# The seam between mixer and MLP: when the MLP's weights are fetched, and where its first tile is normalised

## The chip, the cores and the metric

The kernel runs on the 8 cores of one Trainium2 chip, as one program with other data on each core; cores don't talk to each other. A core takes half of one sequence: 4096 output tokens, with 2064 tokens of lookback. The metric is device time in microseconds, of the slowest core. Of a core's engines, TensorE (PE) multiplies matrices, ScalarE (ACT) and VectorE (DVE) do pointwise work and empty PE's eight PSUM banks, GpSimd (POOL) does pointwise work in SBUF alone and issues the DMAs that convert f32 weights to bf16, and SyncE (SP) issues all other DMAs. Each engine takes its instructions in the order in which they were written; they wait for one another by semaphores.

## The reference

```
h = rms_norm(x, norm_mix_g)
a_b, a_c, a_v, q, k, v, g_a, g_b = split(h @ w_in)
y_a = (a_b * causal_dwconv(a_c * a_v)) @ w_proj_a
y_b = dilated_window_attention(q, k, v) @ w_proj_b      # 12 heads, three dilations
x = x + (sigmoid(g_a + b_0) * y_a + sigmoid(g_b + b_1) * y_b) @ w_out
h = rms_norm(x, norm_ffn_g)
gate, val = split(causal_dwconv(h @ w_up))              # 3 taps, 2 x 2816 channels
x = x + (silu(gate) * val) @ w_down
out = rms_norm(x, final_norm_g)
```

Here x is (4, 8192, 1024) in f32, w_up is 1024 x 5632 and w_down 2816 x 1024.

## The kernel before

The program has three stages: attention with its projections, the mixer's rest, and the MLP. The last two run over the same nine token tiles: one of 388 tokens (4 of them lookback), three of 384 and five of 512 (`BW`; `BB[j]` are tile j's blocks of 128 tokens).

**The mixer's rest**, for each tile j: `conv_c` for four channel chunks, then `gate_oc` for eight output chunks oc. One `gate_oc` is 26 matmuls (L652) into four PSUM banks, two sigmoids on ACT (L1217), two multiplies on DVE (L1231) and a sum into mT on POOL (L1234). Then `wout` multiplies mT with w_out (L1263), DVE adds x (L1267), and SP stores the sum to `x1_d` in HBM (L1271). Tiles overlap: the first conv chunk of tile j+1 is written ahead of `wout(j)`. The last tile, j = 8, has nothing behind its `wout`.

**The MLP**, for each tile: 22 times `c_pair` (up-projection of a gate and a value chunk, 2 x 8 matmuls, L652 by the helper `fm`; ACT scales with the bias, L1411; DVE adds the two other taps, L1418; silu on ACT, L1429, written one pair late; product on POOL, L1431, into `actT`), then `c_down` (L1469) for each block, first k = 0 to 19 of both halves, then k = 20 and 21. Seven buffers tmpC go round among the pairs. The input of a tile is normalised in three steps for each block: `c_stat` (square on ACT, L417, and 1/sqrt in six small steps on POOL, L322 to L330), `c_mul` (DVE, L425, which frees the buffer xn for SP's next load of x1, L1344), and `c_back` (eight transposes on PE, L437, and one copy on DVE, L441, into h2T). For tiles 1 to 8 these steps are hooks within the tile before; for tile 0 they stand ahead of the loop, behind the load and the scaling of g2 (L1330, L335), and behind them stand load and scaling of g3 and the loads of x1 for `c_down` (L1381).

**Weights and memory.** The MLP's weights stay in SBUF: w_up in eleven pieces wU0 to wU10, each two DMAs of 512 KB (as bf16) by `wu_load` (L1162); w_down in three pieces wD0 to wD2 (k = 0 to 7, 8 to 15, 16 to 21) by `wd_load` (L310). All are issued by POOL. SBUF is one arena in which later buffers are laid over earlier ones; `Sched` makes the first user of a buffer wait for the last users of all that lay there. wU0 to wU2 are loaded in tile 1. wU3 to wU5 lie over the conv weights and are issued in tile 8 after its last `conv_c`; wU6 to wU9 lie over the gate weights, and wU6 to wU10 are issued after the last `gate_oc` of tile 8; wD0 to wD2 lie over w_proj_a, w_proj_b, w_out and mT and are issued after `wout(8)`. actT lies over the attention's output and over the buffers xB from which x1 is stored.

Of the kernel before, what the change touches and what calls it, by code (L numbers as in the profile page):

```python
# [8 lines left out]
F32 = mybir.dt.float32  # L9
BF16 = mybir.dt.bfloat16  # L10
# [4 lines left out]
D = 1024  # L15
KC = 8
# [114 lines left out]
def build_program():  # L131
# [94 lines left out]
    R1 = 0  # L226
# [927 lines left out]
    wu_off = [R4, R4 + 8192, R4 + 16384, R1, R1 + 8192, R1 + 16384, R2, R2 + 8192, R2 + 16384, R2 + 24576, R5]  # L1154
# [13 lines left out]
    def wd_load(p):  # L1168
        k0, kn = wd_k[p]
        wD[p] = buf("wD%d" % p, R3 + k0 * 2048, [128, kn, D], BF16)  # L1170
        wload(wD[p], w_dn[k0 * 128:(k0 + kn) * 128, :].rearrange("(k p) c -> p k c", p=128), ("wD%d" % p,))
# [103 lines left out]
    for _ in range(4):  # L1275
        xb_load()
    conv_c(0, 0)
    for j in range(9):
        for c in range(1, 4):
            conv_c(j, c)  # L1280
        if j == 0:
            while ub_b[0] < len(BB[0]) + 1:
                tickno[0] += 1
                ub_step(True)
        if j == 8:
            for p in (3, 4, 5):
                wu_load(p)
        if j == 1:
            for p in (0, 1, 2):
                wu_load(p)  # L1290
        for oc in range(8):
            gate_oc(j, oc)
        b_done[0] = j
        if j + 1 < 9:
            need_b = 1 + sum(len(BB[q]) for q in range(j + 2))
            if j + 2 < 9:
                hb_load(j + 2)
            conv_c(j + 1, 0)
            wout(j)
            while ub_b[0] < need_b:  # L1300
                tickno[0] += 1
                ub_step(True)
        else:
            for p in (6, 7, 8, 9, 10):
                wu_load(p)
            wout(j)
    while deferred:
        tickno[0] += 1
        for d in list(deferred):
            if d[0] <= tickno[0]:  # L1310
                deferred.remove(d)
                d[1]()
    for p in range(3):
        wd_load(p)


    actT = buf("actT", W, [128, 22, 512], BF16)
    tmpC = [buf("tmpC%d" % i, W + 22528 + i * 2048, [128, 512], F32) for i in range(4)]
    h2T = buf("h2T", W + 31232, [128, KC, 512], BF16)
# [4 lines left out]
    g3b = buf("g3b", W + 68096, [128, D], F32)  # L1324
    tmpC += [buf("tmpC%d" % (4 + i), W + 72192 + i * 2048, [128, 512], F32) for i in range(3)]
# [4 lines left out]
    S.add("sp", lambda e: e.dma_start(out=g2b, in_=g2_d.partition_broadcast(128)), writes=[("g2b",)], dma_sem=sem_g2)  # L1330
    scale_g(g2b, ("g2b",))
    tmp_set["n"] = 7
# [162 lines left out]
    xn_load()  # L1495
    xn_load()
    for _ in range(1 + len(BB[0])):
        c_stat()
        c_mul()
        c_back()  # L1500
    S.add("sp", lambda e: e.dma_start(out=g3b, in_=g3_d.partition_broadcast(128)), writes=[("g3b",)], dma_sem=sem_g3)
    scale_g(g3b, ("g3b",))
    for _ in range(3):
        xr_load()
    for j in range(9):
        if j > 0:
            c_corr(j)
        for p in range(22):
            c_pair(j, p)
            if j + 1 < 9 and p in (11, 15):  # L1510
                c_stat()
            if j + 1 < 9 and p in (13, 17):
                c_mul()
# [186 lines left out]
```

How the kernel before makes its waits and increments, by code:

```python
    def emit_stream(ename, handle, tail=None):  # L1587
        waited = {}
        for op in S.ops[ename]:
            need_ = {}
            for d in op.deps:
                sem, val = d.ev
                if waited.get(id(sem), 0) < val and need_.get(id(sem), (None, 0))[1] < val:
                    need_[id(sem)] = (sem, val)
            for sem, val in need_.values():
                handle.wait_ge(sem, val)
                waited[id(sem)] = val
            ins = op.fn(handle)
            if op.dma_sem is not None:
                ins.then_inc(op.dma_sem, 16)
            elif op.signal:
                ins.then_inc(op.ev[0], 1)
        if tail:
            for sem, val in tail:
                handle.wait_ge(sem, val)
```

## Time and profile before

| what | value |
|---|---|
| median of 3 runs | 2178.29 us (2174.97 to 2178.88) |
| profiled execution | 2176.07 us |
| its span, slowest core (7) | 2174.5 us |
| spans of the 8 cores | 2160.0 to 2174.5 us |
| mean granted clock of the cores | 0.975 to 0.979 |
| PE busy | 2000.5 us (92%) |
| DVE, ACT, POOL busy | 1231.0, 859.3, 687.1 us |

The span runs from the first to the last instruction of the slowest core. The views used below are: the page, which cuts the span into 40 slices of 54.4 us with busy shares in tenths; the timeline of one engine, in which equal instructions are merged and the idle time before a row stands in brackets with what ended it; windows, with busy time of each engine in a stretch, the granted TensorE clock (1.0 is 2.4 GHz, 0.5 is 1.2 GHz), the share of the DMA engines and GB/s; the waits, who waited for whom; the chain, which goes back from the last instruction to what released each step; and the DMA views.

### The profile page before, as it was taken

The page shows a single profiled execution, that of the slowest core. Times are in us where ns is not written, and L with a number is a line of the kernel's source. Part 1 is how long each engine was busy: PE and PEld are TensorE (multiplying, and loading weights), DVE is VectorE, ACT ScalarE, POOL GpSimd, SP SyncE. Part 2 cuts the span into 40 slices and gives each one's busy share as a digit, 9 for nine tenths or more (in the row PEclk, how much of TensorE's full clock was granted, in tenths as well). Part 3 has the DMA queues.
Part 4 walks back from the last instruction along what each step waited for, and adds up shares of the span by engine and source line. Part 5 has one row for each costly group of instructions (what it writes and reads, how often), then busy time and mean ns, then how long its engine had stood idle before and what let it go on. Part 6 is the DMA issues. An engine that isn't in the chain of part 4 may idle for free.

```text
span 2174.5 us, 38060 instructions; the slowest of 8 cores (2160.0 to 2174.5 us)
## 1 busy us (share of the span) xinstructions
PE 2000.5 (92%) x11550; PEld 1038.2 (48%) x11550; DVE 1231.0 (57%) x1948; ACT 859.3 (40%) x1796; POOL 687.1 (32%) x1434
## 2 busy tenths in 40 slices
PE   3889989958999999999996499999999999999998
PEld 1546645534555544444442255555544444444443
DVE  5546665455444445344342387686777676858583
ACT  2456654452122221211211264464555453636261
POOL 4333251032111110111122244454545343535342
PEclk9999999988999999999998699999999999999999
DMA  9775857595372223123066921212010202020201
GB/s 182 147 150 146 187 155 124 115 181 143 108 151 74 72 72 127 36 92 105 1 133 111 199 54 69 69 37 71 30 69 30 88 20 97 21 97 20 78 2 49
DMA packets 124160, 201.70 MB, mean 93 GB/s; under 512 B 9620, under 2 KB 86170, under 8 KB 123576
## 3 DMA queue, kind: packets, MB, share of 16 engines
q1 hardware_dynamic: 81912, 164.99, 26.2%
q0 software_dynamic: 42048, 34.26, 12.1%
q8 instruction: 98, 1.61, 0.3%
q14 instruction: 102, 0.84, 0.1%
HBM read 172.86 MB, written 60.63 MB: 107 GB/s over the span
## 4 chain that ended last, share of the span: by engine, by line
PE 81%; DVE 5%; issue 5%; DMA 3%; POOL 2%; ACT 2%; SPq 1%; DVEq 0%; POOLq 0%; ACTq 0%
PE ps L652 56%; PE ps L1469 13%; PE ps L1263 5%; PE ps L658 3%; PE ps L437 1%; PE ps L528 1%; DVE arena L425 1%; DMA u_d<-arena 1%; DMA arena<-x_loc 1%; PE ps L553 1%; DMA arena<-v_d 1%; PE ps L1106 1%; DVE arena L1092 1%; POOL rtmp L328 1%; ACT arena L417 1%
## 5 line engine op out<-in xcount | busy, mean ns | idle before, releaser
L652 PE MATMUL ps<-arena 128*128 128x512 bf16 (+4 forms) x6848 | 1348.9, 357 | 6.5 <-ACT arena L255 4.3
L652 PEld LDWEIGHTS ps<-arena 128*128 128x128 bf16 x6848 | 659.3, 98 | 648.1 <-issue 16.8
L1418 DVE SCALAR_TENSOR_TENSOR arena<-ps,fcw_s,arena 128x511 f32<-128x511 f32 (+4 forms) x792 | 525.0, 687 | 106.3 <-ACT uc L1409 29.8
L1469 PE MATMUL ps<-arena 128*128 128x512 bf16 x1408 | 311.3, 379 | 4.4 <-POOL arena L1422 2.8
L1411 ACT ACTIVATE arena<-ps,fcb_s,fcw_s 128x512 f32<-128x512 f32 (+1 forms) x396 | 284.6, 731 | 0.3 <-ACT uc L1409 0.2
L1431 POOL TENSOR_TENSOR arena<-arena 128x512 bf16<-128x512 bf16 (+1 forms) x198 | 210.5, 1063 | 96.1 <-ACT uc L1409 60.5
L417 ACT ACTIVATE arena<-arena 128x1024 bf16<-128x1024 f32 (+1 forms) x114 | 119.9, 1052 | 299.5 <-DVE arena L1475 205.1
L1231 DVE TENSOR_TENSOR arena<-ps,arena 128x512 f32<-128x512 f32 (+2 forms) x144 | 90.6, 632 | 247.2 <-PE ps L652 240.3
L1469 PEld LDWEIGHTS ps<-arena 128*128 128x128 bf16 x1408 | 136.2, 98 | 166.6 <-issue 9.7
L1217 ACT ACTIVATE arena<-ps,bg_s 128x512 f32<-128x512 f32 (+2 forms) x144 | 92.1, 640 | 264.2 <-PE ps L652 264.2
L1234 POOL TENSOR_TENSOR arena<-arena 128x512 bf16<-128x512 f32 (+2 forms) x72 | 83.3, 1157 | 276.9 <-DVE arena L1231 243.0
L1429 ACT ACTIVATE arena<-arena 128x512 bf16<-128x512 f32 (+1 forms) x198 | 115.2, 582 | 113.1 <-POOL arena L1422 96.4
L425 DVE SCALAR_TENSOR_TENSOR arena<-arena,rstd 128x1024 bf16<-128x1024 f32 (+1 forms) x82 | 105.0, 1280 | 78.0 <-POOL rstd L330 77.7
L1422 POOL TENSOR_TENSOR arena<-arena,corr 128x2 f32<-128x2 f32 x352 | 84.3, 242 | 202.5 <-DVE arena L1418 190.8
L531 ACT ACTIVATE arena<-ps 128x512 bf16<-128x512 f32 x192 | 109.9, 595 | 79.0 <-PE ps L553 45.7
L255 ACT ACTIVATE arena<-ps 128x512 bf16<-128x512 f32 (+4 forms) x157 | 85.8, 548 | 135.2 <-PE ps L652 88.1
L437 PE MATMUL ps<-ident,arena 128*128 128x128 bf16 (+2 forms) x656 | 53.0, 227 | 92.2 <-DVE arena L425 55.5
L322 POOL TENSOR_SCALAR ssq<-ssq 128x1 f32<-128x1 f32 (+1 forms) x106 | 24.9, 235 | 347.6 <-ACT arena L417 297.2
L658 PE MATMUL ps<-arena 128*128 128x256 bf16 (+2 forms) x688 | 119.4, 322 | 1.3 <-DVE arena L441 1.3
L535 DVE TENSOR_TENSOR arena<-arena,mask 128x512 bf16<-128x512 bf16 x160 | 75.0, 476 | 80.1 <-ACT arena L531 78.5
L1263 PE MATMUL ps<-arena 128*128 128x512 bf16 (+1 forms) x528 | 117.7, 382 | 2.5 <-POOL arena L1234 2.5
L1475 DVE TENSOR_TENSOR arena<-ps,arena 128x512 f32<-128x512 f32 x64 | 44.1, 690 | 131.4 <-PE ps L1469 125.2
(89 smaller groups left out, 1276.5 us busy)
## 6 DMA issues: line engine op xcount, KB each, us to landing
arena<-x_loc SPq DMA_DIRECT2D x80, 512.0 KB, 5.4
arena<-x_d SPq DMA_DIRECT2D x64, 512.0 KB, 3.8
x_d<-arena SPq DMA_DIRECT2D x32, 512.0 KB, 4.8
out<-arena SPq DMA_DIRECT2D x32, 512.0 KB, 2.7
u_d<-arena SPq DMA_DIRECT2D x96, 132.0 KB, 5.8
arena<-u_d SPq DMA_DIRECT2D x32, 396.0 KB, 3.6
arena<-w_up POOLq DMA_DIRECT2D x22, 512.0 KB, 17.9
arena<-w_in POOLq DMA_DIRECT2D x10, 1024.0 KB, 22.4
```

What stands on the lines that cost most here:

```text
L417: S.add("act", lambda e: e.activation(out=junk[0:n, :], in_=xap[0:n, :], func=AF.Square, accum_out=ssq[0:n, col:col + 1]), reads=[xkey] + ...
L425: S.add("dve", lambda e: e.scalar_tensor_tensor(out=hbap[0:n, :], in0=xap[0:n, :], scalar=rstd[0:n, col:col + 1], in1=gb[0:n, :], op0=ALU. ...
L531: S.add("act", lambda e: e.activation(out=PA[pi], in_=ps[sbk], func=AF.Exp, scale=0.125), reads=[("ps", sbk)], writes=[("PA%d" % pi,)])
L652: S.add("pe", lambda e, kc=kc: e.matmul(out, lhsT=wap[:, kc, col0:col0 + 128], rhs=rhs(kc), start=(kc == 0), stop=(kc == kcn - 1), skip_gr ...
L658: S.add("pe", lambda e, kc=kc: e.matmul(out, lhsT=lhs(kc), rhs=wap[:, kc, c0:c0 + n], start=(kc == 0), stop=(kc == KC - 1), skip_group_che ...
L1217: S.add("act", lambda e, b=b, t=t, br=br: e.activation(out=tmp[t][:, 0:w_], in_=ps[b][:, 0:w_], func=AF.Sigmoid, bias=bg[:, br * 8 + oc:br ...
L1263: S.add("pe", lambda e, b=b, kc=kc, hf=hf: e.matmul(ps[b][0:n, :], lhsT=mT[:, kc, c0:c0 + n], rhs=wO[:, kc, hf * 512:(hf + 1) * 512], star ...
L1411: S.add("act", lambda e, b=b, t=t, ch=ch, w2_=w2_: e.activation(out=tmpC[t][:, 0:n], in_=ps[b][:, o:w_], func=AF.Identity, scale=w2_, bias ...
L1418: S.add("dve", lambda e, b=b, t=t, sh=sh, wv_=wv_, lo=lo: e.scalar_tensor_tensor(out=tmpC[t][:, lo:n], in0=ps[b][:, o + lo - sh:w_ - sh], ...
L1429: S.add("act", lambda e: e.activation(out=actT[:, p, 0:n], in_=tmpC[tg][:, 0:n], func=AF.Silu), reads=[("tmpC%d" % tg,)], writes=[("actT", ...
L1431: S.add("pool", lambda e: e.tensor_tensor(out=actT[:, p, 0:n], in0=actT[:, p, 0:n], in1=tmpC[tv][:, 0:n], op=ALU.mult), reads=[("tmpC%d" % ...
L1469: S.add("pe", lambda e, b=banks[hf], k_=k_, kk=kk, wt=wt, hf=hf: e.matmul(ps[b], lhsT=actT[:, k_, bi * 128:(bi + 1) * 128], rhs=wt[:, kk, ...
```

## The change

The buffers and helper functions of the MLP's normalisation are defined ahead of the mixer's loop, so that tile 8 can call them. h2T moves to R5, where tile 7's input lay; wU10 moves to where tile 8's input lay; g3b and two tmpC move. In tile 8, g2 and the first two parts of x1 are loaded after the last `conv_c`, and the normalisation of the MLP's tile 0 is spread over the `gate_oc` calls: after chunk 1 g2 is scaled and two `c_stat` run, after chunk 2 two `c_mul`, and so on by the list of letters (s, m and b for `c_stat`, `c_mul` and `c_back`). wU6 and wU7 are issued after chunk 4, wU8 to wU10 and wD0 after chunk 7, wD1 and wD2 after `wout(8)`. g3 and the x1 blocks for `c_down` are loaded after pair 3 of the MLP's tile 0, and g3 is scaled after pair 20. The bodies of the functions that move are as they were.

```diff
-    wu_off = [R4, R4 + 8192, R4 + 16384, R1, R1 + 8192, R1 + 16384, R2, R2 + 8192, R2 + 16384, R2 + 24576, R5]
+    wu_off = [R4, R4 + 8192, R4 + 16384, R1, R1 + 8192, R1 + 16384, R2, R2 + 8192, R2 + 16384, R2 + 24576, W + 31232]
...
+    actT = buf("actT", W, [128, 22, 512], BF16)
+    tmpC = [buf("tmpC%d" % i, W + (68096 + i * 2048 if i < 5 else 26624 + (i - 5) * 2048), [128, 512], F32) for i in range(7)]
+    h2T = buf("h2T", R5, [128, KC, 512], BF16)
+    hbC = [buf("hbC%d" % i, W + 39424 + i * 2048, [128, D], BF16) for i in range(2)]
+    g2b = buf("g2b", W + 43520, [128, D], F32)
+    xn = [buf("xn%d" % i, W + 47616 + i * 4096, [128, D], F32) for i in range(2)]
+    xr = [buf("xr%d" % i, W + 55808 + i * 4096, [128, D], F32) for i in range(3)]
+    g3b = buf("g3b", W + 22528, [128, D], F32)
+    sem_g2, sem_g3 = newsem("s_g2"), newsem("s_g3")
+    sem_xn = [newsem("s_xn%d" % i) for i in range(2)]
+    sem_xr = [newsem("s_xr%d" % i) for i in range(3)]
+    sem_out = [newsem("s_out%d" % i) for i in range(3)]
+    xn_list = [(0, -1)] + [(j, b) for j in range(9) for b in BB[j]]
+    xn_l, cf, cb = [0], [0], [0]
...
@@ -1285,11 +1349,22 @@
         if j == 8:
             for p in (3, 4, 5):
                 wu_load(p)
+            S.add("sp", lambda e: e.dma_start(out=g2b, in_=g2_d.partition_broadcast(128)), writes=[("g2b",)], dma_sem=sem_g2)
+            xn_load()
+            xn_load()
         if j == 1:
             for p in (0, 1, 2):
                 wu_load(p)
         for oc in range(8):
             gate_oc(j, oc)
+            if j == 8:
+                if oc == 1:
+                    scale_g(g2b, ("g2b",))
+                if oc == 4:
+                    wu_load(6)
+                    wu_load(7)
+                for k_ in ("", "ss", "mm", "bbs", "ms", "bm", "b", "")[oc]:
+                    {"b": c_back, "m": c_mul, "s": c_stat}[k_]()
         b_done[0] = j
...
         else:
-            for p in (6, 7, 8, 9, 10):
+            for p in (8, 9, 10):
                 wu_load(p)
+            wd_load(0)
             wout(j)
...
-    for p in range(3):
-        wd_load(p)
-
-
-    actT = buf("actT", W, [128, 22, 512], BF16)
-    tmpC = [buf("tmpC%d" % i, W + 22528 + i * 2048, [128, 512], F32) for i in range(4)]
-    h2T = buf("h2T", W + 31232, [128, KC, 512], BF16)
-    hbC = [buf("hbC%d" % i, W + 39424 + i * 2048, [128, D], BF16) for i in range(2)]
-    g2b = buf("g2b", W + 43520, [128, D], F32)
-    xn = [buf("xn%d" % i, W + 47616 + i * 4096, [128, D], F32) for i in range(2)]
-    xr = [buf("xr%d" % i, W + 55808 + i * 4096, [128, D], F32) for i in range(3)]
-    g3b = buf("g3b", W + 68096, [128, D], F32)
-    tmpC += [buf("tmpC%d" % (4 + i), W + 72192 + i * 2048, [128, 512], F32) for i in range(3)]
-    sem_g2, sem_g3 = newsem("s_g2"), newsem("s_g3")
-    sem_xn = [newsem("s_xn%d" % i) for i in range(2)]
-    sem_xr = [newsem("s_xr%d" % i) for i in range(3)]
-    sem_out = [newsem("s_out%d" % i) for i in range(3)]
-    S.add("sp", lambda e: e.dma_start(out=g2b, in_=g2_d.partition_broadcast(128)), writes=[("g2b",)], dma_sem=sem_g2)
-    scale_g(g2b, ("g2b",))
+    wd_load(1)
+    wd_load(2)
     tmp_set["n"] = 7
...
-    xn_load()
-    xn_load()
-    for _ in range(1 + len(BB[0])):
-        c_stat()
-        c_mul()
-        c_back()
-    S.add("sp", lambda e: e.dma_start(out=g3b, in_=g3_d.partition_broadcast(128)), writes=[("g3b",)], dma_sem=sem_g3)
-    scale_g(g3b, ("g3b",))
-    for _ in range(3):
-        xr_load()
     for j in range(9):
         if j > 0:
             c_corr(j)
         for p in range(22):
             c_pair(j, p)
+            if j == 0 and p == 3:
+                S.add("sp", lambda e: e.dma_start(out=g3b, in_=g3_d.partition_broadcast(128)), writes=[("g3b",)], dma_sem=sem_g3)
+                for _ in range(3):
+                    xr_load()
+            if j == 0 and p == 20:
+                scale_g(g3b, ("g3b",))
```

## Rows read from the trace of the kernel before

**Rows 1.** The page's slices: TensorE's granted clock in 40 slices of 54.4 us.

```profile
PEclk9999999988999999999998699999999999999999
```

**Rows 2.** PE timeline, 1080 to 1300: start, duration, instruction, count, idle before and its end.

```profile
1101.36 60.60 PE L652 MATMUL ps<-arena 128*128 128x512 bf16 x280
1164.48 15.44 PE L1263 MATMUL ps<-arena 128*128 128x512 bf16 x64 [2.52 <-POOL arena L1234]
1208.15 0.35 PE L437 MATMUL ps<-ident,arena 4*128 4x4 bf16 x8 [28.23 <-DVE arena L425]
...
1227.11 1.01 PE L437 MATMUL ps<-ident,arena 128*128 128x128 bf16 x8 [3.28 <-DVE arena L425]
1229.07 60.13 PE L652 MATMUL ps<-arena 128*128 128x388 bf16 x352 [0.94 <-DVE arena L441]
1289.22 4.26 PE L1469 MATMUL ps<-arena 128*128 128x512 bf16 x19
1294.08 5.36 PE L1469 MATMUL ps<-arena 128*128 128x512 bf16 x23 [0.60 <-POOL arena L1431]
```

**Rows 3.** Windows: stretch, length, busy PE, PEld, DVE, ACT, POOL, clock, DMA share, GB/s.

```profile
1140.00:1160.00 20.00, 20.00 (x94) 9.11 (x93) 4.46 (x7) 4.91 (x8) 5.05 (x4) 1.00 0.19 27
...
1200.00:1230.00 30.00, 4.32 (x36) 3.06 (x37) 7.38 (x8) 2.30 (x4) 9.24 (x26) 0.50 1.14 179
```

**Rows 4.** Waits, 1160 to 1230: who waited for what, total us, times, longest.

```profile
ACT arena L335 <- DMA arena<-g: 31.6, 1, 31.6
ACT arena L417 <- DMA arena<-x_d: 25.1, 3, 21.2
```

**Rows 5.** The chain, 1180 to 1420: start, duration, what.

```profile
1211.56 9.90 DMA arena<-x_d
...
1244.30 40.96 PE ps L652 x248
...
1299.44 0.47 PE ps L437 x8
```

**Rows 6.** POOL timeline, 1080 to 1240: DMA issues and one sum.

```profile
1120.10 5.31 POOL L1162 DMA_DIRECT2D arena<-w_up  x6 [0.55 <-issue]
...
1146.13 1.26 POOL L1234 TENSOR_TENSOR arena<-arena 128x512 bf16<-128x512 f32 x1 [4.35 <-DVE arena L1231]
...
1164.17 6.18 POOL L1162 DMA_DIRECT2D arena<-w_up  x7
1176.85 1.76 POOL L1162 DMA_DIRECT2D arena<-w_up  x2 [6.50 <-issue]
1194.78 0.88 POOL L1162 DMA_DIRECT2D arena<-w_up  x1 [16.17 <-issue]
...
1202.33 1.71 POOL L310 DMA_DIRECT2D arena<-w_dn  x2 [5.79 <-issue]
```

**Rows 7.** DMA queues, 1164.2 to 1262.2: q0 POOL's, q1 SP's; packets, MB, share.

```profile
q0 software_dynamic: 13264, 11.01, 83.7%
q1 hardware_dynamic: 2024, 7.36, 23.2%
```

**Rows 8.** Line L310, 1195 to 1205: the three w_dn pieces.

```profile
DMA to landing us min/median/max: 40.7/51.6/59.0
```

**Rows 9.** Line L1162, 1119 to 1126: the six pieces of wU3 to wU5.

```profile
DMA to landing us min/median/max: 7.7/15.3/19.8
```

**Rows 10.** Line L1344, 1180 to 1229: loads of x1.

```profile
DMA to landing us min/median/max: 8.4/9.9/12.1
```

**Rows 11.** Line L1271, 1165 to 1183: the last four stores of x1.

```profile
DMA to landing us min/median/max: 7.9/8.1/10.0
```

**Rows 12.** DVE timeline, 1180 to 1296: its first and last work in MLP tile 0.

```profile
1239.97 3.11 DVE L1418 SCALAR_TENSOR_TENSOR arena<-ps,fcw_s,arena 128x384 f32<-128x384 f32 x5 [11.05 <-ACT uc L1409]
...
1287.75 8.81 DVE L1418 SCALAR_TENSOR_TENSOR arena<-ps,fcw_s,arena 128x384 f32<-128x384 f32 x14
```

**Rows 13.** Lines, DVE, 1229 to 1297: group, count, busy us, mean ns, idle before.

```profile
L1418 DVE SCALAR_TENSOR_TENSOR arena<-ps,fcw_s,arena 128x384 f32<-128x384 f32 x87 | 50.0, 613 | 15.9 <-ACT uc L1409 11.1 <-DVE arena L1418 0.5
```

More of the change, by code:

```diff
@@ L1273, in wout @@
             later(3, xb_load)
[L1275 to L1303, printed above, removed]
-            for p in (6, 7, 8, 9, 10):
[L1305 to L1312, printed above, removed]
-    for p in range(3):
-        wd_load(p)
     actT = buf("actT", W, [128, 22, 512], BF16)
-    tmpC = [buf("tmpC%d" % i, W + 22528 + i * 2048, [128, 512], F32) for i in range(4)]
-    h2T = buf("h2T", W + 31232, [128, KC, 512], BF16)
+    tmpC = [buf("tmpC%d" % i, W + (68096 + i * 2048 if i < 5 else 26624 + (i - 5) * 2048), [128, 512], F32) for i in range(7)]
+    h2T = buf("h2T", R5, [128, KC, 512], BF16)
     hbC = [buf("hbC%d" % i, W + 39424 + i * 2048, [128, D], BF16) for i in range(2)]
@@ L1329, in build_program @@
     sem_out = [newsem("s_out%d" % i) for i in range(3)]
-    S.add("sp", lambda e: e.dma_start(out=g2b, in_=g2_d.partition_broadcast(128)), writes=[("g2b",)], dma_sem=sem_g2)
-    scale_g(g2b, ("g2b",))
-    tmp_set["n"] = 7
     xn_list = [(0, -1)] + [(j, b) for j in range(9) for b in BB[j]]
@@ L1382, in xr_load @@
               reads=[("x1_d", blk)], writes=[("xr%d" % sl, 0), ("xr%d" % sl, 1)], dma_sem=sem_xr[sl])
+    for _ in range(4):
+        xb_load()
+    conv_c(0, 0)
+    for j in range(9):
+        for c in range(1, 4):
+            conv_c(j, c)
+        if j == 0:
+            while ub_b[0] < len(BB[0]) + 1:
+                tickno[0] += 1
+                ub_step(True)
+        if j == 8:
+            for p in (3, 4, 5):
+                wu_load(p)
+            S.add("sp", lambda e: e.dma_start(out=g2b, in_=g2_d.partition_broadcast(128)), writes=[("g2b",)], dma_sem=sem_g2)
+            xn_load()
+            xn_load()
+        if j == 1:
+            for p in (0, 1, 2):
+                wu_load(p)
+        for oc in range(8):
+            gate_oc(j, oc)
+            if j == 8:
+                if oc == 1:
[5 more added lines that the diff above has]
+                    {"b": c_back, "m": c_mul, "s": c_stat}[k_]()
+        b_done[0] = j
+        if j + 1 < 9:
+            need_b = 1 + sum(len(BB[q]) for q in range(j + 2))
+            if j + 2 < 9:
+                hb_load(j + 2)
+            conv_c(j + 1, 0)
+            wout(j)
+            while ub_b[0] < need_b:
+                tickno[0] += 1
+                ub_step(True)
+        else:
+            for p in (8, 9, 10):
+                wu_load(p)
+            wd_load(0)
+            wout(j)
+    while deferred:
+        tickno[0] += 1
+        for d in list(deferred):
+            if d[0] <= tickno[0]:
+                deferred.remove(d)
+                d[1]()
+    wd_load(1)
+    wd_load(2)
+    tmp_set["n"] = 7
     fw = fcw.rearrange("p (c k) -> p c k", k=3)
```

## The prediction

> **What bounds the kernel now.** I read the page's slices first: TensorE's (PE's) granted clock stands at nine tenths or more but for two places, slices 9 and 10 (in the attention, which the change leaves alone) and slices 22 and 23, where the digits fall to 8 and 6 [rows 1]. Then PE's own timeline of the second place. The last mixer tile's output projection (L1263) ends at 1164.48 + 15.44 = 1179.92 us, and the first matmul of the MLP (L652) starts at 1229.07: 49.15 us in which PE does only four small groups of transposes [rows 2]. Third, the windows: from 1200 to 1230 PE is busy 4.32 of 30 us and its granted clock is 0.50, which is the 1.2 GHz level; in the gates of the last mixer tile (1140 to 1160) PE is full while VectorE (DVE), ScalarE (ACT) and GpSimd (POOL) are each busy about 5 of 20 us [rows 3]. Fourth, the waits of 1160 to 1230: ACT waits 31.6 us for one load of g2 and 25.1 us for loads of x1, and all else queues behind that [rows 4]. So the hole is a serial prologue (load, square, rstd, multiply, transpose) that starts only after the mixer has ended, with its loads in the thick of the weight stream. Nothing after the hole waits for anything else: the first down-projection starts at 1289.22, straight behind the last up-projection [rows 2].
>
> **The change, part by part.** The sum is made against the profiled execution (span 2174.5 us, 2176.07 us with what lies around it).
>
> *The prologue leaves the hole.* It moves between the gates of tile 8, where the three helper engines are three quarters idle. With its result in h2T before the output projection, the MLP's first matmul needs wU0 (loaded in tile 1), h2T and a free PSUM bank, so it can follow L1263 at once: minus 49.15 us. The transposes stay PE work: three groups of eight at 0.47 us at full clock [rows 5], and the four-row group at 0.35 at most (that was at half clock) [rows 2]: plus 1.8 us.
>
> *The clock.* PE restarted cold in 1229. At full clock 248 matmuls of tile 0 took 40.96 us, 0.1652 each [rows 5]; 352 of them make 58.1 us where 60.15 passed from 1229.07 to 1289.22 [rows 2]. Minus 2.0 us. The small wait of 2.52 us ahead of L1263 stays.
>
> *What the moved steps wait for in tile 8.* One output chunk of the gates is 26 of the 280 matmuls of 60.60 us, 5.63 us [rows 2]; chunk 2 ends at about 1134, chunk 3 at 1139.5, chunk 5 at 1151, chunk 6 at 1157. x1 blocks 1 and 2 are loaded once the first two multiplies have freed xn, at about 1136 and 1137.3. In the hole such loads landed after 8.4 to 12.1 us beside the weight stream [rows 10], and from a landing (1211.56 + 9.90) to the transposes (1227.11) 5.65 us passed [rows 2, 5]. So block 1 is ready for PE at 1150 to 1154, against PE's arrival at 1151.5; block 2, with four wU issues of 0.9 us [rows 6] ahead of it on POOL, by 1158.6 at the latest, against 1157.6. PE waits 0 to 3 us; I take 1. Queued behind ACT's wait for block 1 are the sigmoids of chunk 4, up to 6 us late; PE has eight banks, two chunks or 11 us, before it notices. On POOL the sum for mT of chunk 5 slips by 2 to 4 us, needed only at the output projection. On SP nothing is due between the xn loads and the stores of 1170. With that cover gone (loads over 15 us late) the whole delay would stand on PE.
>
> *The weight stream.* Before: wU6 to wU10 and wD0 to wD2 are issued from 1164.17 on, POOL being held up three times (at 1170, 1178 and 1196, the last issue at 1203.2) [rows 6], and the last piece lands 59.0 us after that, at 1262.2 [rows 8]; that was hidden, since the down-projection began at 1289. After, it begins at 1240, so this cover shrinks to nothing and the stream has to be sized. From 1164.2 to 1262.2 the POOL queue moved 11.01 MB and SP's queue 7.36 MB [rows 7], together 187 GB/s. After: wU6 and wU7 (2.1 MB) are issued behind the sum at 1146.13 [rows 6], when the stream of wU3 to wU5 (last landing 19.8 us after 1124.5, [rows 9]) is over, and are through by about 1166 to 1169. From there remain 8.9 MB of weights; of SP's 7.36 MB the loads of g2 and of five x1 blocks (3.1 MB) are gone from this stretch, leaving 4.2. 13.1 MB at 187 GB/s are 70 us: the last piece lands at 1236 to 1239. It is needed at k = 16 of the first down-projection: 1181.7 + 58.1 + 3.5 = 1243.3. Zero, with 4 to 7 us to spare. The bounds: at the 131 GB/s of the w_up pieces alone (six of 0.52 MB in 24.3 us, [rows 6, 9]) it lands at 1269 and costs 26 us; no bound below zero, since an earlier landing gains nothing. I take zero because 187 is the rate of just this mix.
> The Trainium skill speaks for the other end. "DMA: Bandwidth & Descriptors", section "Anatomy of one DMA", has a POOL-issued transfer cost 2 us plus its bytes at 436 GB/s; worked out from that as an estimate, the 13.1 MB would be through 30 us after 1166, at 1196. The trace does not agree (187 GB/s in this mix), and the measurement decides; by the page the first rival below would have no chance at all.
>
> *POOL's queue.* The order of the 13 pieces is unchanged. Before, seven went out one behind another, and then POOL was held up before the eighth, tenth and twelfth [rows 6]: seven under way seem to be what the queue takes. After, pieces 1 to 4 are through by 1169, so wU10 and wD0 go out by then, and wD1 and wD2 when L1263 has ended, about 1182 to 1184, with seven under way at most. Behind them on POOL stands the first gate product of the MLP, not due before 1188. Zero; if a piece held POOL until 1197, seven tmpC buffers and eight banks (eight pairs, 21 us) would hide it.
>
> *The start of the MLP.* Its first silu writes actT over xB and so waits for the last x1 store; stores landed after 7.9 to 10.0 us [rows 11], the last one issued near 1182.6, so by 1192.6, when ACT could have gone on at 1187. Before, ACT waited too (for g3): DVE's first operation came at 1239.97, 10.9 us after PE's start, and it then worked to 1287.75 + 8.81 = 1296.56 nearly without a gap (87 x 0.613 us) [rows 12, 13]; the price was 0.60 us on PE [rows 2]. After, DVE starts 3 us behind PE, pauses 5, but PE is 2 us faster: about as far behind at the end. g3's load and scaling come later and are needed only at the end of the down-projection. Bounds 0 to 3 us more than before; I take 0.5.
>
> **Sum:** -49.15 + 1.8 - 2.0 + 1.0 + 0.5 = -47.85 us. The profiled execution would take 2128.2; its 2176.07 stands 2.2 under the median 2178.29, which would become 2130.4 us.
>
> **Rivals.**
> *1. The weights come late.* PE then stands at k = 0, 8 or 16 of the first down-projection until wD0, wD1 or wD2 lands. For it: the slack is 4 to 7 us in 74; that wU6 and wU7 don't get ahead, because loads of x1 share their stretch, is the way in which the change would not do what it says. Against: the rate used already contains waits of POOL. At 160 GB/s the last piece lands at 1250, 7 us late: 2138. At the bound of 131: 2156.
> *2. The hooks hold PE in tile 8.* Loads of x1 at 12 us or more, one behind another, with the square, the rstd chain and the wU issues in order on ACT and POOL: 3 to 10 us, and PE's clock falls for a while: 2133 to 2141. For it: the bare 0 to 1 us of margin above. Against: PE's eight banks, and engines a quarter busy.
> *3. No gain: the chain only moves.* That needs a transfer which ends the hole whatever comes before it. The only candidate, the stream, ended 27 us ahead of the down-projection (1262.2 against 1289.2), so at least that part of the hole is not the stream's. 2178.
> *4. Slower.* The stream beside the kernel's own stores falls well below what rows show on the whole: if the 8.9 MB of weights and 4.2 MB of the rest go at under 105 GB/s, the last piece lands 125 us after 1166, at 1291 or later, PE stands 48 us in the first down-projection, goes cold there, and the gain is used up: at 95 GB/s 138 us, 61 us late, about 2191. Nothing but short stretches of the profile runs so low.
>
> **How the numbers follow.** Forecast 0.74 (2126 to 2134), rival 1 0.14 (2134 to 2156, mostly to 2142), rival 2 0.07, rival 3 0.015, rival 4 0.025, and 0.01 for a better end than the forecast's. The range 2124 to 2141 holds the forecast and the likelier part of rivals 1 and 2: its low end is the longest step saved with no stall at all, and the ordinary spread of runs. About 0.2% is what can be told from no change: faster 0.96, same 0.015, slower 0.025.
>
> **What would show it.** PE's timeline must have L652 straight behind L1263, with four groups of L437 among the gates and no gap over 3 us there; the granted clock at 1.0 from the first L652 of the MLP on; 352 matmuls of tile 0 in 58 us; the first L1469 about 60 us after the end of L1263, with idle time before it put down to DVE or POOL, not to w_dn. The POOL rows must show w_up issues near 1147, and the last w_dn landing before the first down-projection. A wait of L1469 for a DMA means rival 1; idle time of PE before L437 or L652 in tile 8 means rival 2. If the hole is gone and the time is not lower by 40 us or more, the forecast is wrong.

## The result, and the profile after

The changed kernel takes 2125.08 us (median of 4 runs, 2122.13 to 2130.84) against 2178.59 us (4 runs, 2174.97 to 2179.42) for the kernel before: ratio 0.9761, 95% interval 0.9735 to 0.9786. That is 5.3 us under the predicted 2130.4 and inside the range of 2124 to 2141. The comparisons here and below leave out the runs in which one half of the chip was disturbed.

The profiled execution took 2122.13 us, its span 2120.6 us on the slowest core (core 1); the eight cores spanned 2109.4 to 2120.6 us. PE is busy 1994.3 us, 94% of the span, and the granted clock of the cores is 0.989 to 0.991, where it was 0.975 to 0.979. In the page's slices, clock and busy share of PE, the dip of slices 22 and 23 [rows 1] is gone, and the one at slices 9 and 10 stands as before:

```profile
PEclk9999999988999999999999999999999999999999
...
PE   3899989967999999999999999999999999999998
```

The seam in PE's timeline of core 1 (start, duration, instruction, count, in brackets the idle time before and what ended it). Line numbers have moved: the down-projection is L1479 (L1469 before), the taps on DVE are L1428 (L1418), the silu L1439 (L1429), the product L1441 (L1431), the loads of x1 into xn L1299 (L1344).

```profile
1094.25 38.15 PE L652 MATMUL ps<-arena 128*128 128x512 bf16 x176
1132.33 0.90 PE L437 MATMUL ps<-ident,arena 4*128 4x4 bf16 x16
1133.07 11.39 PE L652 MATMUL ps<-arena 128*128 128x512 bf16 x52
1144.29 0.61 PE L437 MATMUL ps<-ident,arena 128*128 128x128 bf16 x8
1144.74 5.78 PE L652 MATMUL ps<-arena 128*128 128x512 bf16 x26
1150.86 0.61 PE L437 MATMUL ps<-ident,arena 128*128 128x128 bf16 x8 [0.34 <-DVE arena L425]
...
1159.53 15.66 PE L1263 MATMUL ps<-arena 128*128 128x512 bf16 x64 [2.46 <-POOL arena L1234]
1175.03 57.95 PE L652 MATMUL ps<-arena 128*128 128x388 bf16 x352
1232.82 3.62 PE L1479 MATMUL ps<-arena 128*128 128x512 bf16 x16
1238.68 7.46 PE L1479 MATMUL ps<-arena 128*128 128x512 bf16 x26 [2.25 <-DMA arena<-w_dn]
```

The hole of 49.15 us [rows 2] is gone: L652 of the MLP stands straight behind L1263. Its transposes lie among the gates and waited once on this core, for 0.34 us. The 352 matmuls of tile 0 take 57.95 us with no idle time, where 60.13 were needed [rows 2]. The last row is new: k = 16 to 21 of the first block waits 2.25 us for the last piece of w_down. The same stages as windows (length, busy PE, PEld, DVE, ACT, POOL, clock, DMA share, GB/s):

```profile
1130.00:1150.00 20.00, 20.00 (x113) 9.57 (x111) 10.22 (x12) 6.89 (x11) 12.52 (x20) 1.00 1.02 179
...
1175.00:1232.80 57.80, 57.80 (x353) 34.44 (x352) 46.98 (x80) 38.55 (x106) 23.30 (x33) 1.00 1.09 195
1232.80:1245.00 12.20, 9.95 (x40) 4.15 (x38) 6.64 (x12) 4.68 (x11) 3.67 (x4) 0.86 0.12 41
```

The gates that had DVE, ACT and POOL at about 5 of 20 us [rows 3] now carry the prologue with them at 10.2, 6.9 and 12.5, and PE is still full. In the third row PE stood for a DMA, and the granted clock, which is a mean over the window, falls to 0.86.

A profile is one core of one execution, so I took the seam from the PE timelines of all eight cores: the time from the end of L1263 to the first up-projection of MLP tile 1. Before it is 138.7 to 144.3 us, mean 141.7 (hole 49.2, up-projection 61.7, down-projection 30.8); after it is 87.5 to 94.2, mean 89.4 (-0.2, 57.9, 31.7; the ends of matmuls are modelled, so neighbouring rows can overlap a little). The gates of tile 8 up to L1263 took 63.1 us on every core before and 64.8 to 66.9 after. So 52.3 us are saved behind the mixer and on average 2.6 given back inside it. The rest of the MLP is unchanged (854.5 and 853.8 us).

### The profile page after: what moved, and what is told of

Read it like the earlier page. It is cut to its first block, busy times and chain, and to the rows that moved or that the text cites. A ratio compares the mean times of both kernels' runs of the same rounds, so it can differ in the third digit from the quotient of the medians.

```text
span 2120.6 us, 38053 instructions; the slowest of 8 cores (2109.4 to 2120.6 us)
## 1 busy us (share of the span) xinstructions
PE 1994.3 (94%) x11550; PEld 1036.0 (49%) x11550; DVE 1234.9 (58%) x1948; ACT 858.1 (40%) x1796; POOL 687.1 (32%) x1434
## 4 chain that ended last, share of the span: by engine, by line
PE 83%; DVE 5%; issue 4%; DMA 3%; POOL 2%; ACT 2%; DVEq 0%; SPq 0%; POOLq 0%; another core or an unknown queue 0%; ACTq 0%
PE ps L652 56%; PE ps L1479 14%; PE ps L1263 5%; PE ps L658 3%; PE ps L528 1%; PE ps L437 1%; DMA u_d<-arena 1%; DVE arena L425 1%; DVE arena L1092 1%; PE ps L553 1%; DMA arena<-x_loc 1%; DMA arena<-v_d 1%; DVE arena L1428 1%; PE ps L1106 1%; DVE ssq L322 1%
## 5 line engine op out<-in xcount | busy, mean ns | idle before, releaser
L652 PE MATMUL ps<-arena 128*128 128x512 bf16 (+4 forms) x6848 | 1343.7, 356 | 1.1 <-DVE arena L441 1.1
L652 PEld LDWEIGHTS ps<-arena 128*128 128x128 bf16 x6848 | 658.1, 98 | 637.7 <-issue 4.0
L1428 DVE SCALAR_TENSOR_TENSOR arena<-ps,fcw_s,arena 128x511 f32<-128x511 f32 (+4 forms) x792 | 525.0, 687 | 100.9 <-ACT arena L1421 24.7
L1479 PE MATMUL ps<-arena 128*128 128x512 bf16 x1408 | 312.8, 380 | 5.4 <-POOL arena L1432 2.8
L1441 POOL TENSOR_TENSOR arena<-arena 128x512 bf16<-128x512 bf16 (+1 forms) x198 | 210.4, 1062 | 86.0 <-ACT uc L1419 47.1
L1479 PEld LDWEIGHTS ps<-arena 128*128 128x128 bf16 x1408 | 136.8, 98 | 168.1 <-issue 12.2
L1439 ACT ACTIVATE arena<-arena 128x512 bf16<-128x512 f32 (+1 forms) x198 | 115.2, 582 | 112.3 <-POOL arena L1432 96.0
L1263 PE MATMUL ps<-arena 128*128 128x512 bf16 (+1 forms) x528 | 117.9, 383 | 2.5 <-POOL arena L1234 2.5
L1419 ACT ACTIVATE uc<-ps 128x2 f32<-128x2 f32 x396 | 66.3, 167 | 125.2 <-PE ps L652 124.2
```

Source lines behind the costliest of these rows:

```text
L652: S.add("pe", lambda e, kc=kc: e.matmul(out, lhsT=wap[:, kc, col0:col0 + 128], rhs=rhs(kc), start=(kc == 0), stop=(kc == kcn - 1), skip_gr ...
L1263: S.add("pe", lambda e, b=b, kc=kc, hf=hf: e.matmul(ps[b][0:n, :], lhsT=mT[:, kc, c0:c0 + n], rhs=wO[:, kc, hf * 512:(hf + 1) * 512], star ...
L1428: S.add("dve", lambda e, b=b, t=t, sh=sh, wv_=wv_, lo=lo: e.scalar_tensor_tensor(out=tmpC[t][:, lo:n], in0=ps[b][:, o + lo - sh:w_ - sh], ...
L1439: S.add("act", lambda e: e.activation(out=actT[:, p, 0:n], in_=tmpC[tg][:, 0:n], func=AF.Silu), reads=[("tmpC%d" % tg,)], writes=[("actT", ...
L1441: S.add("pool", lambda e: e.tensor_tensor(out=actT[:, p, 0:n], in0=actT[:, p, 0:n], in1=tmpC[tv][:, 0:n], op=ALU.mult), reads=[("tmpC%d" % ...
L1479: S.add("pe", lambda e, b=banks[hf], k_=k_, kk=kk, wt=wt, hf=hf: e.matmul(ps[b], lhsT=actT[:, k_, bi * 128:(bi + 1) * 128], rhs=wt[:, kk, ...
```

## The experiments

The theory: what is saved is the hole and PE's cold restart, and the part of it that is lost is lost at w_down, whose last piece now comes a few us late. The rival: the weights cost nothing, and what differs from the sum lies elsewhere (the wait for g3, the clock). Each ratio is to the kernel before on the same chip.

**Is the prologue or the weights the gain?** In this kernel the prologue is spread over tile 8 as in the change, but the weights go out at the times of before.

```diff
                 if oc == 4:
-                    wu_load(6)
-                    wu_load(7)
...
-            for p in (8, 9, 10):
+            for p in (6, 7, 8, 9, 10):
                 wu_load(p)
-            wd_load(0)
             wout(j)
...
-    wd_load(1)
-    wd_load(2)
+    for p in range(3):
+        wd_load(p)
```

> The changed kernel, but with wU6 to wU10 issued after the last gate chunk and all of w_dn after the mixer, as in the kernel before: only the prologue is moved. Theory (the prologue is the gain, and the earlier weights keep the stream from becoming the next wait): the hole is gone, the stream ends some 13 us later (2.1 MB at about 165 GB/s), PE stands 12 to 18 us ahead of or within the first down-projection: 2136 to 2145. Rival A (the stream still has slack): 2125 to 2128. Rival B (the earlier weights are most of the gain): over 2160.

Measured (prologue_alone): 2139.8 us, ratio 0.9839 (0.9811 to 0.9868). The last w_down piece landed 75.7 to 80.7 us after the mixer's end. The time is what lateness predicts, yet PE stood mostly in another place. PE of the slowest core, 6:

```profile
1179.24 21.18 PE L652 MATMUL ps<-arena 128*128 128x388 bf16 x128
1211.75 38.59 PE L652 MATMUL ps<-arena 128*128 128x388 bf16 x224 [11.33 <-DVE arena L1424]
...
1258.84 3.57 PE L1475 MATMUL ps<-arena 128*128 128x512 bf16 x8 [5.05 <-POOL arena L1437]
```

PE does eight pairs (128 matmuls) and then waits 11.33 us within the up-projection, long before w_down is due. The last row's wait is put down to POOL, but it ends as the last w_down piece lands, at 1258.6; the seven other cores name w_dn there. POOL of the same core:

```profile
1165.12 6.26 POOL L1162 DMA_DIRECT2D arena<-w_up  x7
...
1183.55 1.75 POOL L1162 DMA_DIRECT2D arena<-w_up  x2 [12.18 <-issue]
...
1199.35 0.88 POOL L1162 DMA_DIRECT2D arena<-w_up  x1 [14.05 <-issue]
...
1206.74 1.70 POOL L310 DMA_DIRECT2D arena<-w_dn  x2 [5.64 <-issue]
1208.46 3.55 POOL L1437 TENSOR_TENSOR arena<-arena 128x384 bf16<-128x384 bf16 x4
```

The waits of that stretch on core 6 (who for whom, total us, times, longest):

```profile
ACT arena L1417 <- POOL arena L1437: 14.7, 1, 14.7
...
PE ps L652 <- DVE arena L1424: 11.3, 1, 11.3
```

POOL takes seven pieces, then stands at "issue" until pieces land, three times, to 1208. The first gate product stands behind those issues, so no tmpC comes free, ACT waits 14.7 us for one, DVE has nothing to finish and PE no bank. The chain of waits names DVE, two engines from the cause. Over the eight cores PE waits 7.2 to 16.4 us in the two places together, where 12 to 18 had been expected.

**The same lateness, with POOL free.** As the last kernel, with the last five pieces issued between the pairs of tile 0.

```diff
-            for p in (6, 7, 8, 9, 10):
+            for p in (6, 7, 8):
                 wu_load(p)
...
-    for p in range(3):
-        wd_load(p)
...
+            if j == 0 and p in (2, 5):
+                wu_load({2: 9, 5: 10}[p])
+            if j == 0 and p in (8, 10, 12):
+                wd_load((p - 8) // 2)
```

> As the run with the prologue alone, but wU9 to wD2 are issued one by one after pairs 2, 5, 8, 10 and 12 of the MLP's tile 0, so that POOL never stands before a full queue (it did for 14 us, and PE for 7 to 14 us in the up-projection behind it). Theory (the loss of that run is the lateness of the last piece, and PE's stand in the up-projection only took a part of it beforehand): the up-projection takes 58 to 60 us, PE then waits 12 to 18 us for w_dn in the first down-projection, the time stays at 2136 to 2143. Rival (POOL's stand is the loss): 2125 to 2130.

Measured (spread_late): 2142.83 us, ratio 0.9831 (0.98 to 0.9863). PE on core 1:

```profile
1175.64 63.25 PE L652 MATMUL ps<-arena 128*128 128x388 bf16 x352
...
1246.88 3.24 PE L1473 MATMUL ps<-arena 128*128 128x512 bf16 x8 [6.27 <-DMA arena<-w_dn]
...
1254.31 8.52 PE L1473 MATMUL ps<-arena 128*128 128x512 bf16 x26 [4.18 <-DMA arena<-w_dn]
```

PE no longer stands in the up-projection, and the loss is at w_down. Which engine stands, and where, depends on who is held by the issues; how much is lost depends on when the last piece lands: 75.1 to 78.3 us after the mixer here, 75.7 to 80.7 in prologue_alone, and from the mixer's end to tile 1 both take the same on average over the cores, 105.2 and 105.6 us. Two sizes were missed. The up-projection took 63.1 to 63.9 us on cores 0 to 3 and 68.0 to 68.6 on the others, not 58 to 60, which has a cause of its own (the clock, last section); and since PE arrives later by that, it waits only 3.3 to 10.5 us for w_dn, not 12 to 18.

**The weights early, the prologue late.** The g2 and x1 loads and the steps of the prologue leave tile 8, and g3 and the xr loads stand where they stood before; the diff shows a part of it.

```diff
...
                 if oc == 4:
                     wu_load(6)
                     wu_load(7)
-                for k_ in ("", "ss", "mm", "bbs", "ms", "bm", "b", "")[oc]:
-                    {"b": c_back, "m": c_mul, "s": c_stat}[k_]()
...
+    S.add("sp", lambda e: e.dma_start(out=g2b, in_=g2_d.partition_broadcast(128)), writes=[("g2b",)], dma_sem=sem_g2)
+    scale_g(g2b, ("g2b",))
+    xn_load()
+    xn_load()
+    for _ in range(1 + len(BB[0])):
+        c_stat()
+        c_mul()
+        c_back()
...
```

> The weights as in the changed kernel (wU6 and wU7 after chunk 4, wD0 ahead of the output projection), but the whole prologue with its loads stands after the mixer, as before. Theory (the hole is the serial prologue; the stream lengthens it, by meeting its loads and by holding POOL's rstd steps behind DMA issues until 24 us after the mixer's end): the hole stays, but POOL is free, so it shrinks from 49 to about 35 us: 2157 to 2170. Rival A (the hole is the prologue alone, the stream is nothing to it): 2176 to 2180. Rival B (the weights are the gain): under 2150.

Measured (weights_alone): 2174.8 us, ratio 0.9972 (0.9953 to 0.999); 2157 to 2170 had been expected. The hole shrank from 45.6 to 51.7 us only to 38.2 to 41.6. PE on core 3:

```profile
1158.28 15.64 PE L1263 MATMUL ps<-arena 128*128 128x512 bf16 x64 [2.52 <-POOL arena L1234]
...
1192.07 0.35 PE L437 MATMUL ps<-ident,arena 4*128 4x4 bf16 x8 [18.15 <-DVE arena L425]
...
1212.89 12.33 PE L652 MATMUL ps<-arena 128*128 128x388 bf16 x64 [0.94 <-DVE arena L441]
```

Less of the stream lies beside the prologue's loads, and the first transpose comes 18.15 us after L1263 instead of 28.23 [rows 2]; but the rest of the chain is serial work of ACT, POOL and DVE. On this chip cores 4 to 7 ran at a granted clock of 0.81 for part of the time; of cores 0 to 3 the slowest took 2162.1 us (median of the runs) against 2173.5 for the kernel before there, which is inside what was expected. In mean spans the weights alone save 9.8 us on those cores and 6.9 on all, the prologue alone 35.0 (2168.3 to 2133.3), and both 46.9 on the chip of prologue_alone: the prologue brings the gain, and the early weights are worth about 12 us to it, more than without it.

**What the wait for g3 was worth in the kernel before.** Only g3, its scaling and the three xr loads move, as in the change.

```diff
-    S.add("sp", lambda e: e.dma_start(out=g3b, in_=g3_d.partition_broadcast(128)), writes=[("g3b",)], dma_sem=sem_g3)
-    scale_g(g3b, ("g3b",))
-    for _ in range(3):
-        xr_load()
...
+            if j == 0 and p == 3:
+                S.add("sp", lambda e: e.dma_start(out=g3b, in_=g3_d.partition_broadcast(128)), writes=[("g3b",)], dma_sem=sem_g3)
+                for _ in range(3):
+                    xr_load()
+            if j == 0 and p == 20:
+                scale_g(g3b, ("g3b",))
```

> The kernel before, with nothing changed but that g3 and the x1 blocks for the first down-projection are loaded after pair 3 and g3 is scaled after pair 20 of the MLP's tile 0. It asks why tile 0 took 60 to 62 us in the kernel before and 57.8 after. Theory of the prediction (PE's cold clock after the hole): nothing changes, 2178 +- 1, tile 0 still over 60 us. Rival (ACT, which had to scale g3 before it could empty the first PSUM bank, let PE run out of banks): tile 0 at 59 us or less, 1 to 3 us faster, 2175 to 2177.

Measured (g3_alone): ratio 0.9999 (0.998 to 1.0018). In the time of the slowest core nothing shows, and cores 0 to 3 span the same as before; cores 4 to 7 span 3.1 us less on average (2164.3 against 2167.4). In the trace it shows. PE of the kernel before on core 4:

```profile
1217.55 12.56 PE L652 MATMUL ps<-arena 128*128 128x388 bf16 x64 [0.94 <-DVE arena L441]
...
1231.82 47.73 PE L652 MATMUL ps<-arena 128*128 128x388 bf16 x288 [1.71 <-DVE arena L1418]
```

and of this kernel on core 7:

```profile
1223.09 60.39 PE L652 MATMUL ps<-arena 128*128 128x388 bf16 x352 [0.94 <-DVE arena L441]
1283.31 9.23 PE L1469 MATMUL ps<-arena 128*128 128x512 bf16 x42
```

Seven of the eight cores of before took 61.0 to 62.3 us for tile 0, six of them with a wait of 0.9 to 1.8 us for DVE in it, which started late because ACT waited for g3. Core 0 (61.0) and the prediction's core, 7, with its 60.15, had no such wait. With g3 late no core has it. Cores 4 to 7 then take 60.2 to 60.7 (cores 0 to 3 take 62.0 to 63.2, with 14.8 us at a granted clock of 0.81): the cold restart is worth about 2.4 us (60.3 against 57.9), g3's wait 0 to 2 us, and the 0.60 us ahead of L1469 [rows 2] belonged to it too.

**Is w_down late because of SP's loads?** The x1 load for the first `c_down` block goes behind pair 16, g3 and the other two behind pair 21, each held by the pair it names (SP waits for nothing else and would issue them at once); g3 is scaled after the first `c_down` block, which the diff leaves out.

```diff
-            if j == 0 and p == 3:
-                S.add("sp", lambda e: e.dma_start(out=g3b, in_=g3_d.partition_broadcast(128)), writes=[("g3b",)], dma_sem=sem_g3)
-                for _ in range(3):
-                    xr_load()
-            if j == 0 and p == 20:
-                scale_g(g3b, ("g3b",))
+            if j == 0 and p == 16:
+                xr_load([("actT", 14)])
...
+        if j == 0:
+            S.add("sp", lambda e: e.dma_start(out=g3b, in_=g3_d.partition_broadcast(128)), reads=[("actT", 20)],
+                  writes=[("g3b",)], dma_sem=sem_g3)
+            xr_load()
+            xr_load()
```

> The changed kernel, but the four SP loads of g3 and of x1 for the first down-projection (2.1 MB), which go out straight behind the last x1 stores, are held back until late in the MLP's tile 0. Theory (the weight stream ends only just in time, and these loads delay it): the last w_dn piece lands 8 to 12 us earlier against the end of the mixer, no core waits for w_dn in the first down-projection, 2 to 4 us less than the changed kernel: 2121 to 2123. Rival (the stream has its own pace, whatever SP loads beside it): it lands as before, 2125.

The unchanged kernel beside it on the same chip:

> The changed kernel once more, beside the three others on the same chip. About 2125 us (2121 to 2131). On some cores PE should wait 2 to 7 us for a w_dn piece in the first down-projection, on others not at all.

Measured: held (held_loads) 0.9781 (0.9752 to 0.9811), unchanged (after_again) 2126.67 us, 0.9778 (0.9751 to 0.9805). Held, the last piece lands 53.4 to 59.0 us after the mixer, unchanged 60.3 to 65.3: about 7 us sooner, where 8 to 12 had been expected. Held, no core waits for it; unchanged, cores 5 to 7 wait 2.1 to 3.1 us. The slowest core shows none of this, because cores 0 to 3 spent 26 to 33 us of tile 0 at a granted clock of 0.81 there. Both ran again on a third chip (after_third, held_again), with the kernel before beside them (before_again).

> The changed kernel on the same chip. 2122 to 2130. If the chip shows stretches at 0.81: on some cores 25 to 35 us of them between the end of the mixer and the first down-projection, and an up-projection of tile 0 of 62 to 64 us against 57.8 on cores without; by the theory about as much as in the kernel before, by the rival much more.

> The loads of g3 and x1 held back, beside the changed kernel on the same chip. No wait for w_dn; on cores without stretches at 0.81, 87.6 us from the MLP's start to its second tile against 88 to 94 in the changed kernel. In time 0 to 3 us less than the changed kernel; if it is not less by more than the intervals, the stand at w_dn is no longer what sets the end.

> The kernel before, profiled on the chip on which the two next are run. In the runs so far some pairs of cores had stretches with a granted clock of 0.81 in the MLP's tile 0 while PE was full. Theory (it belongs to the chip and to this stage, in whatever kernel): a chip that shows it shows it here too, 10 to 30 us of it on the same cores, with the up-projection of tile 0 at 62 to 64 us on them; 2178. Rival (it comes with the change, since PE now runs full through the weight stream): none here, and on the same cores some in the changed kernel.

Measured: unchanged 2127.8 us, 0.9767 (0.9737 to 0.9798); held 2124.84 us, 0.9753 (0.9719 to 0.9786); before 1.0003 (0.9975 to 1.003). PE of the unchanged kernel on core 6:

```profile
1240.07 7.41 PE L1479 MATMUL ps<-arena 128*128 128x512 bf16 x26 [5.02 <-DMA arena<-w_dn]
```

and of held on core 7, where no wait is left:

```profile
1181.74 57.95 PE L652 MATMUL ps<-arena 128*128 128x388 bf16 x352
1239.53 9.23 PE L1479 MATMUL ps<-arena 128*128 128x512 bf16 x42
```

Line L310 on core 7, the three w_down pieces from issue to landing, unchanged:

```profile
DMA to landing us min/median/max: 48.3/51.2/61.8
```

and held, with about 7 us less for each:

```profile
DMA to landing us min/median/max: 41.4/43.4/54.5
```

The slowest cores don't part the two kernels (the intervals overlap), but the mean spans do. On cores 4 to 7, which had no stretch at 0.81 in the profiles of these two chips, the held kernel spans 2115.5 and 2116.6 us against 2121.3 and 2120.0 unchanged (five runs each): 3.4 and 5.8 us less, each with a standard error near 2, so the two together show it and the smaller alone would not. The traces agree: from the mixer's end to tile 1 cores 4 to 7 of the third chip take 87.5 to 88.9 us held and 90.0 to 94.3 unchanged. On cores 0 to 3 the mean span is 2122.6 and 2120.0 against 2121.5 and 2121.3: nothing. So the late piece costs what the theory says where the clock is left alone; as a better kernel the held one is not shown.

**Can the 2.46 us ahead of L1263 be filled?** The first pair of the MLP is written ahead of `wout(8)`, once in the changed kernel and once in the held one.

```diff
+            tmp_set["n"] = 7
+            c_pair(0, 0)
             wout(j)
...
-            c_pair(j, p)
+            if j > 0 or p > 0:
+                c_pair(j, p)
```

> The changed kernel, but pair 0 of the MLP (16 matmuls, 2.6 us) is written ahead of the last tile's output projection, where PE waits 2.46 us for POOL's last sum and its clock then falls for 3.4 us. Theory: the wait and the fall go, 3 to 4 us on every core, 2120 to 2123. Rival (the pair's ACT and DVE work delays what frees the banks of the output projection, so the wait moves): 2125 to 2128.

> Pair 0 ahead of the output projection, and the loads of g3 and of x1 for the first down-projection held back. Theory: both act, no wait of PE over 1 us from the gates of the mixer's last tile to the second tile of the MLP: 5 to 8 us under the changed kernel, 2117 to 2122. Rival (what is gained in the seam is lost in the spread of the cores ahead of it): 2122 to 2127.

Measured: 2141.6 us, 0.9823 (0.9798 to 0.9849), for the first (pair_early), and 2135.7 us, 0.9784 (0.976 to 0.9809), for the second; 2117 to 2123 had been expected of the two. PE of the first on core 0:

```profile
1157.00 8.40 PE L652 MATMUL ps<-arena 128*128 128x512 bf16 x41
1165.24 13.98 PE L1263 MATMUL ps<-arena 128*128 128x512 bf16 x63
...
1192.78 7.38 PE L652 MATMUL ps<-arena 128*128 128x388 bf16 x44 [1.75 <-DVE arena L1373]
```

and ACT there:

```profile
1188.39 1.28 ACT L1384 ACT_TABLE_LOAD   x1 [7.03 <-DMA x_d<-arena]
```

The wait ahead of L1263 is gone and comes back 25 us later: ACT reaches its first silu one pair sooner, waits 7.03 us for the store of x1 and PE runs out of banks (1.75 us here, 0.9 to 3.6 on the other cores). Cores 0 to 3 span 2119.8 us on average, within the 2116.9 to 2121.5 of the changed kernel in its three sets of runs: no gain. That the whole program is slower comes from cores 4 to 7 of that chip (2133.1 us), with up to 155 us at a granted clock of 0.81; the changed kernel was not run on it, so whether it would show the same stays open.

## Why the prediction was right, point by point

**The hole, -49.15: right.** L652 follows L1263 on every core. The weights alone leave 38 to 42 us of it, the prologue alone fills it.

**Transposes and waits in tile 8, +1.8 and +1.0: right.** They cost 1.7 to 3.8 us, 2.6 on average. On core 1 block 1 made no wait and block 2 one of 0.34 us (over the eight cores 0 to 0.5 and 0 to 1.3), as the loads of x1 landed sooner than the 8.4 to 12.1 us taken from the hole [rows 10] (line L1299 in tile 8, core 1):

```profile
DMA to landing us min/median/max: 4.8/7.2/7.3
```

**The clock, -2.0: the right mechanism, a size read from the wrong core.** 57.95 us came for 58.1. What was too small is the time before: I took 60.15 from core 7, the slowest, and seven of eight cores took 61.0 to 62.3. The step is worth 3.2 to 4.5 us there, of which g3_alone gives about 2.4 to the cold restart and, on the six cores that have it, most of the rest to ACT's wait for g3, which the prediction priced at 0.60.

**The weight stream, "zero, with 4 to 7 us to spare": the term that was mis-sized.** The rate was right and the bytes were not. The DMA queues of core 1 from the landing of wU7 (1161.7) to the last landing (packets, MB, rate; then packets, MB, share):

```profile
DMA packets 10527, 14.24 MB, mean 186 GB/s; under 512 B 304, under 2 KB 6423, under 8 KB 10519
...
q0 software_dynamic: 9079, 8.90, 83.9%
q1 hardware_dynamic: 1440, 5.24, 20.4%
```

187 GB/s and 8.9 MB of weights were forecast and came, and wU7 was through 13.5 us ahead of the mixer's end, as forecast. SP's queue moved 5.24 MB and not 4.2: the sum left out two x1 loads for later normalisation (tile 1's last block and tile 2's first). In the kernel before they came 14 us behind the stream's end of 1262.2; with the MLP 50 us sooner they fall into it. SP on core 7 before, then on core 1 after:

```profile
1276.73 11.49 SPq L1344 DMA_DIRECT2D arena<-x_d  x2
...
1218.99 11.49 SPq L1299 DMA_DIRECT2D arena<-x_d  x2
```

1.05 MB more are 5.6 us at 186 GB/s (an estimate), most of the 6 to 9 us by which the last piece came later than forecast. g3 and the xr loads, which the sum had, were written after pair 3 and went out at 1176, straight behind the stores: SP waits for no pair, so the written place puts them in order on SP's queue and sets no time. The last piece was issued at 1176.8 and landed at 1238.4, 63.2 us after the mixer's end, where k = 16 was reached at 1236.4. On three of eight cores PE waited 2.0 to 3.6 us, and the first down-projection took 33.9 us on core 1 against 29.8 undisturbed, the rest being matmuls at the lower clock after the wait. This is rival 1 in small; held_loads and held_again took it away, and cores 4 to 7 gained 5.8 and 3.4 us.

**POOL's queue, zero: right, and so was its cover.** POOL issued the last pieces without being held beyond L1263:

```profile
1159.22 5.38 POOL L1162 DMA_DIRECT2D arena<-w_up  x6
1164.53 0.94 POOL L310 DMA_DIRECT2D arena<-w_dn  x1
1175.89 1.71 POOL L310 DMA_DIRECT2D arena<-w_dn  x2 [10.42 <-PE ps L1263]
```

The prediction added that a POOL held until 1197, 15 us past the start of the MLP, would be hidden by seven tmpC and eight banks (eight pairs, 21 us). prologue_alone bears that out: there POOL was held to 1208, 29 us past the mixer's end, PE did its eight pairs in 21.18 us, stood, and went on at 1211.75, 3.3 us after POOL had begun its first product (1208.46). So about 18 us of holding are hidden and what lies beyond shows on PE in full: 11.33 us on that core, 6.7 to 13.9 over the eight, and on cores 0, 4, 5 and 7 the same 18 us fit to 0.1 us.

**The start of the MLP, +0.5: nothing was lost.** ACT waited for the store of x1 as forecast, on core 1:

```profile
1183.58 1.28 ACT L1439 ACT_TABLE_LOAD   x1 [3.61 <-DMA x_d<-arena]
```

DVE waited behind it, and PE, in its row of 57.95 us above, did not:

```profile
1186.47 3.83 DVE L1428 SCALAR_TENSOR_TENSOR arena<-ps,fcw_s,arena 128x384 f32<-128x384 f32 x6 [5.05 <-ACT uc L1419]
```

How near that cover is to its end shows in pair_early, where the same wait of ACT lasted 7.03 us and PE stood 1.75.

**The sum.** Forecast -47.85. Mean spans over all cores went from 2168.3 to 2121.4 us (-46.9) on the chip of after_again and from 2168.1 to 2120.6 (-47.5) on that of after_third. Step by step, in the means over the eight cores of before_again and after_third: hole -49.4, gates of tile 8 +2.7, up-projection -2.6, first down-projection +1.7, together -47.6. That the total is met so closely is luck: the weights' 1.7, forecast as zero, is made up for the most part by 0.5 that the start of the MLP did not cost, 0.6 more from the up-projection (the stretches at 0.81 of the last section in it) and 0.3 from the hole and the gates. The time is that of the slowest core, and there the medians fell by 53.5 us in the first comparison, 51.4 with after_again and 50.9 with after_third. The 3 to 5 us between slowest core and mean are not explained by any step: core 7 before entered tile 8 at 1101.36 us and core 1 after at 1094.25, in code that is the same, so where the slowest core stands ahead of the seam is part of it. The interval of the ratio, 5.5 us each way, is as wide.

## What to carry to other kernels

When a hole is filled, everything that the hole had hidden needs sizing again: list the bytes of every queue in the new, shorter window, prefetches for the next tile among them, and take for each load the time at which its queue can issue it, not the place where it is written. Where an engine both issues DMAs and computes, a stand at its DMA issues stops its computing as well, and the profile then blames an engine two steps away. Read each term of the sum on several cores before trusting it: the slowest core of one execution may be the one on which a step was cheap.

## What the runs showed of the hardware

**POOL's DMA issue blocks after seven pieces.** In the kernel before [rows 6] and in prologue_alone thirteen pieces, of 512 KB and more, are written one behind another. Seven go out in 6.2 to 6.3 us. Then POOL waits three times at "issue" and computes nothing meanwhile: 6.5 and 12.2 us before the eighth piece, 16.2 and 14.1 before the tenth, 5.8 and 5.6 before the twelfth (on the slowest core of each). What ends these waits can be read from the landings: on all eight cores of both kernels the eighth piece goes out 0.3 to 0.4 us after the second has landed, the tenth after the fourth and the twelfth after the sixth (core 6 of prologue_alone: 1183.6 behind 1183.2, 1199.4 behind 1199.0, 1206.7 behind 1206.4). POOL is held by the landing of its own earlier pieces, two at a time.

**A granted clock of 0.81 with PE full.** Besides 1.0 and 0.50, which stands for 1.2 GHz, rows show 0.81, which is neither level of the clock, on neighbouring cores at the same time. Windows of tile 0 in the third chip's run of the changed kernel, core 0:

```profile
1183.10:1244.20 61.10, 61.10 (x353) 35.51 (x353) 50.05 (x85) 41.78 (x112) 25.14 (x34) 0.95 1.07 192
...
1216.20:1222.50 6.30, 6.30 (x33) 3.43 (x32) 5.78 (x11) 5.06 (x14) 3.71 (x9) 0.81 1.08 173
1222.80:1231.60 8.80, 8.80 (x56) 5.22 (x54) 8.17 (x14) 6.42 (x18) 4.46 (x7) 1.00 1.07 158
```

and core 7, with no such stretch:

```profile
1173.70:1231.50 57.80, 57.80 (x353) 34.44 (x352) 45.87 (x78) 37.33 (x102) 23.32 (x32) 1.00 1.08 188
```

PE is full before, during and after; 61.1 us instead of 57.8 is what it costs. The first chip showed none of it around the seam, the third 18 to 24 us on cores 0 to 3 with the changed kernel and 6.5 us on the same cores with the kernel before (25 to 35 and 10 to 30 had been expected). The two other chips point the same way: g3_alone, which keeps the hole, had 14.8 us of it on cores on which after_again had 27 to 33, and weights_alone 0 to 9 us where spread_late and pair_early had 30 to 67. So it does not take the change to bring it about, but the kernels in which PE is full through the seam had more of it, which on the third chip gives back 2 to 3 us on those cores (an estimate: 0.19 of the 12 to 18 us by which it is longer). That rests on one profile of each kernel and chip; what sets it off stays open.
